# Expert tables of a decoder step: the second selection matrices move to ScalarE, and one ring of weight units runs through both tables

## The chip, the cores and the metric

The kernel runs on one core of a Trainium2 chip. The metric is the device time of one execution in microseconds; before the change the median of three runs was 3930.49 us (3925.4 to 3931.15).

## The reference

One inference step of one layer, all in fp32: a mixer (retention and gated linear attention) and then a product-key expert block, for 512 prompt tokens and 64 sample tokens. The change lies in the expert block:

```python
v1, i1 = lax.top_k(s1, 16); v2, i2 = lax.top_k(s2, 16)      # 8 heads, two halves of 128 keys
cand_s = v1[..., :, None] + v2[..., None, :]
cand_i = i1[..., :, None] * 128 + i2[..., None, :]
top_s, sel = lax.top_k(cand_s, 16)
eidx = take_along_axis(cand_i, sel)                          # 128 experts per token
gate = softmax(top_s)
act = gelu(einsum('thkd,td->thk', u_tab[eidx], xb))
out = einsum('thk,thkd->td', gate * act, v_tab[eidx])
```

There are 128 x 128 = 16384 experts, each with a row of 2048 numbers in the table u and one in the table v (128 MB a table).

## The kernel before

Of the 576 tokens, 384 are done densely: `experts_hidden` multiplies the whole table u with them, `outputs` the whole table v, and a matrix G of gates (one number for each expert and token, mostly zero) picks what counts. The other 192 tokens are done by gathers: GpSimd fetches the rows of 128 experts at a time with an indirect DMA of 1 MB, 192 gathers for each table.

**Units.** A table comes in 128 units of 1 MB (`Units`, lines 1483 to 1511). SyncE issues a unit's load (L1494), ScalarE rounds it to a high part (`split_hi`, L1501), VectorE forms the low part (`split_lo`, L1505), and TensorE multiplies with 48 matmuls of 384 columns (L1718 to L1720 for u, L2163 to L2165 for v). Two buffers each. Semaphores: `raw_in`, `hi_done`, `lo_done`, `unit_done`.

**First table (`experts_hidden`, names `hidden_...`).** Iteration n of the loop of each engine stands for unit n of 128. Units 0 to 39 go with the choice of the experts (`route`). From unit `first_gate` = 40 on, the gate matrices are built beside the units, 96 groups of 4 tokens: for each token a matrix `hot[1]` that has a one where iota equals the second key (GpSimd, L1662), a matrix `hot[0]` with the gate where iota equals the first key (VectorE, `firsts_hots`, L1930), a matmul of both (`gate_matrices`, L1703, awaits both), and a copy to a staging tile (`stage_gates`, ScalarE, L1759). After 8 groups SyncE stores 2 MB of G (`store_group`, L1606). Function `gate_groups(n)` says which groups unit n has: one, sometimes two. The buffers `hot` are double, so group k waits until group k-2 is multiplied (semaphore `made`). Every matmul group of a unit ends in a Gelu (L1773), whose result SyncE stores (192 KB, L1633), and only then issues the next load.

**Gathers and dots.** In iteration n GpSimd first builds its selection matrices and then issues the unit's gathers (L1649; 22 before unit 40, 170 after it, so one or two per unit), into 4 row buffers; VectorE multiplies each with the token's own row (`dot`, L1922) and so frees the buffer. VectorE's order in iteration n is: low part of unit n+1, `firsts_hots`, dots.

**Second table (`outputs`).** It is a block of its own; all engines meet at the boundary between blocks. SyncE then loads chunk 0 of the hidden values and of G (1.5 MB each, L2023 and L2025) and the first two units of v. VectorE clears the accumulators `acc` and `accg`, waits for the unit, multiplies the hidden chunk with G (L2088, 8 instructions), ScalarE rounds it (L2064, twice), VectorE forms the low part (L2095, twice), and TensorE may begin.

Of the kernel before, what the change touches and what calls it, by code (L numbers as in the profile page):

```python
# [1477 lines left out]
class Units:  # L1478
# [4 lines left out]
    def __init__(self, nc, a, per):  # L1483
        self.nc, self.per = nc, per
# [4 lines left out]
        self.hi_done, self.lo_done, self.done = a.sem("hi_done"), a.sem("lo_done"), a.sem("unit_done")  # L1489

# [6 lines left out]
    def split_hi(self, act, n, s):  # L1497
        act.wait_ge(self.raw_in[s], filled(n, s))

        wait(act, self.done, self.per * (n - 1))  # L1500
# [25 lines left out]
def experts_hidden(nc, name, c, ident, u_units, h_hi, h_lo, hidden, queries, keys, u_rows, h_rows, h_weight, expert_ids, dots, gates0, G):  # L1526
# [9 lines left out]
    first_gate, after_gates = 8 * TILES, NKEYS - 4  # L1536
# [16 lines left out]
    with ExitStack() as ctx:  # L1553
        a = Alloc(nc, ctx, name)
        un = Units(nc, a, 1)
# [6 lines left out]
        big = [a.sb(f"big{n}", [P, NKEYS * GT]) for n in range(2)]  # L1562
# [5 lines left out]
        picks_hot = spare[:].rearrange("p (k j) -> p k j", j=TOPK)  # L1568
        hot = [[spare[:, (2 * n + x) * P:(2 * n + x + 1) * P] for n in range(2 * B)] for x in range(2)]
# [23 lines left out]
            a.sem(x) for x in ("chosen", "back", "kept", "dstep", "ready", "ids_set"))  # L1593
        seconds_hot, firsts_hot, made, staged, row_used, carried, dot_gelu, weighted = (
# [6 lines left out]
        def _(sp):  # L1601
# [66 lines left out]
        def _(pe):  # L1668
# [27 lines left out]
            def gate_matrices(k):  # L1696
# [3 lines left out]
                pe.wait_ge(seconds_hot, B * (k + 1))  # L1700
# [31 lines left out]
        def _(act):  # L1732
# [12 lines left out]
            def keep(t):  # L1745
                act.wait_ge(back, t - 1)
                for n, x in enumerate(choices):
                    nc.scalar.copy(x[:, (t - 2) * P:(t - 1) * P], tg[:, n, :]).then_inc(kept, 1)
# [40 lines left out]
        def _(vec):  # L1789
# [144 lines left out]
            for n in range(NKEYS):  # L1934
                if n + 1 < NKEYS:
                    un.split_lo(vec, n + 1, (n + 1) % 2)
# [49 lines left out]
def outputs(nc, name, v_units, hidden, G, v_rows, expert_ids, dots, acc, accg):  # L1986
# [6 lines left out]
    with ExitStack() as ctx:  # L1993
        a = Alloc(nc, ctx, name)
        un = Units(nc, a, DT)
        gat = Gathers(nc, a, v_rows, expert_ids, NGATHER // (NCH // 2))
        W = a.sb("w", [P, CH, ND])
        Gc = a.sb("g", [P, NG, CH, GT])
# [4 lines left out]
        added, weighed, gated, w_in, w_hi_done, w_lo_done, w_set, cleared = (  # L2003
            a.sem(x) for x in ("added", "weighed", "gated", "w_in", "w_hi_done", "w_lo_done", "w_set", "cleared"))
# [12 lines left out]
        def _(sp):  # L2017
            def load_w(c):
# [3 lines left out]
                at = bass.ds(c, 1)  # L2022
                sp.dma_start(W[:].rearrange("p a t -> p (a t)"),  # L2023
                             hidden[at].rearrange("c p a t -> (c p) (a t)")).then_inc(w_in, 16)
                sp.dma_start(Gc[:].rearrange("p g a t -> p (g a t)"),  # L2025
# [330 lines left out]
```

## Time and profile before

| | |
|---|---|
| median of three runs | 3930.49 us |
| the profiled execution | 3937.12 us, its span 3935.3 us |
| TensorE busy | 3594.5 us (91%), mean granted clock 0.945 |
| VectorE, ScalarE, GpSimd busy | 2579.9, 1118.0, 1360.3 us |
| GpSimd's selection matrices (L1662) | 489.1 us |
| DMA | 965.63 MB, mean 245 GB/s |

Times are microseconds from the span's start. Matmuls overlap, so busy TensorE is not TensorE at its peak. A row of the timeline gives start, length, engine, line, operation, tiles, shapes and count, and in brackets the engine's idle time before it and what ended that.

### The profile page before, as it was taken

How to read it: one execution, taken by the hardware profiler on the slowest of the kernel's cores; microseconds unless marked ns; L12 is line 12 of the kernel's file. 1: busy time of each engine (PE TensorE's matmuls, PEld its weight loads, DVE VectorE, ACT ScalarE, POOL GpSimd, SP SyncE). 2: the span in 40 equal slices, each digit the busy share in tenths (PEclk: the TensorE clock that was granted, in tenths of full speed). 3: DMA queues.
4: the chain of work that ended last, by engine and by line, in shares of the span. 5: the costliest groups of instructions: out<-in, count | busy, mean ns of one | idle time of the engine just before them, and what ended most of it. 6: DMA issues, size and time to landing. Idle time of an engine off the chain costs nothing. (4 is left out here: it accounts for less than half of the span.)

```text
span 3935.3 us, 50012 instructions
## 1 busy us (share of the span) xinstructions
PE 3594.5 (91%) x19479; PEld 3341.1 (85%) x19479; DVE 2579.9 (66%) x3623; ACT 1118.0 (28%) x1130; POOL 1360.3 (35%) x993
## 2 busy tenths in 40 slices
PE   8999997886988989988998999998699999999996
PEld 6888886664877879888998999998699999999995
DVE  4111113885314138998777777777698989898996
ACT  5212112332214123322333333333122222222222
POOL 0000000000000000122978878888155545454451
PEclk9999998777999989998999999999799999999997
DMA  5222222534415143554888888988889898989986
GB/s 203 106 101 98 109 99 74 182 114 157 159 64 216 59 155 139 221 219 186 336 327 338 343 326 321 362 329 339 311 337 372 352 375 348 378 347 377 358 348 228
DMA packets 186998, 965.63 MB, mean 245 GB/s; under 512 B 18657, under 2 KB 61345, under 8 KB 86098
## 3 DMA queue, kind: packets, MB, share of 16 engines
q1 hardware_dynamic: 108082, 506.07, 34.1%
q0 software_dynamic: 61264, 426.27, 28.0%
q10 hardware_dynamic: 17488, 31.06, 2.2%
q8 instruction: 108, 1.77, 0.2%
q14 instruction: 56, 0.46, 0.0%
HBM read 865.77 MB, written 97.55 MB: 245 GB/s over the span
## 5 line engine op out<-in xcount | busy, mean ns | idle before, releaser
L1718 PE MATMUL hidden_hp<-dense_hi,hidden_whi 128*128 128x384 f32 x2048 | 712.8, 348 | 36.2 <-DVE hidden_wlo L1505 36.2
L2163 PE MATMUL outputs_vp<-outputs_w_hi,outputs_whi 128*128 128x384 f32 x2048 | 685.2, 335 | 36.1 <-DVE outputs_w_lo L2095 35.7
L1719 PE MATMUL hidden_hp<-dense_lo,hidden_whi 128*128 128x384 f32 x2048 | 700.0, 342 | 0.0
L1720 PE MATMUL hidden_hp<-dense_hi,hidden_wlo 128*128 128x384 f32 x2048 | 699.0, 341 | 0.0
L2164 PE MATMUL outputs_vp<-outputs_w_lo,outputs_whi 128*128 128x384 f32 x2048 | 684.7, 334 | 0.0
L2165 PE MATMUL outputs_vp<-outputs_w_hi,outputs_wlo 128*128 128x384 f32 x2048 | 684.6, 334 | 0.0
L1922 DVE CUSTOM_DVE_ANT_0 hidden_row<-hidden_row,hidden_h_row 128x2048 f32<-128x2048 f32 x192 | 439.1, 2300 | 157.8 <-DMA hidden_row<-u_rows,expert_ids 155.2
L1662 POOL TENSOR_SCALAR hidden_spare<-hidden_iota,hidden_seconds 128x128 f32<-128x128 f32 x384 | 489.1, 1286 | 133.4 <-PE hidden_tq L1703 88.1
L1649 POOL DMA_INDIRECT hidden_row<-u_rows,expert_ids x192 | 318.4, 1659 | 587.2 <-DVEq L1901 356.2
L1977 POOL DMA_INDIRECT outputs_row<-v_rows,outputs_id x192 | 315.9, 1645 | 554.3 <-DVE accg L2112 513.7
L2112 DVE SCALAR_TENSOR_TENSOR accg<-outputs_row,outputs_w_op,accg 128x2048 f32<-128x2048 f32 x192 | 450.8, 2348 | 52.1 <-DMA outputs_row<-v_rows,outputs_id 49.3
L1501 ACT CAST outputs_whi<-outputs_raw 128x2048 fp32r<-128x2048 f32 x128 | 245.1, 1915 | 794.3 <-PE outputs_vp L2165 643.2
L1718 PEld LDWEIGHTS hidden_hp<-dense_hi,hidden_whi 128*128 128x128 f32 x2048 | 398.3, 194 | 41.1 <-DVE hidden_wlo L1505 40.7
L2163 PEld LDWEIGHTS outputs_vp<-outputs_w_hi,outputs_whi 128*128 128x128 f32 x2048 | 384.9, 188 | 37.2 <-issue 37.0
L1719 PEld LDWEIGHTS hidden_hp<-dense_lo,hidden_whi 128*128 128x128 f32 x2048 | 397.6, 194 | 0.0
L1720 PEld LDWEIGHTS hidden_hp<-dense_hi,hidden_wlo 128*128 128x128 f32 x2048 | 396.1, 193 | 0.0
L2164 PEld LDWEIGHTS outputs_vp<-outputs_w_lo,outputs_whi 128*128 128x128 f32 x2048 | 385.0, 188 | 0.0
L2165 PEld LDWEIGHTS outputs_vp<-outputs_w_hi,outputs_wlo 128*128 128x128 f32 x2048 | 384.9, 188 | 0.0
L542 PE MATMUL in_proj_acc<-in_proj_whi,in_proj_rows_hi 128*128 128x512 f32 x960 | 376.1, 392 | 2.1 <-DVE in_proj_wlo L435 2.1
L1505 DVE TENSOR_TENSOR hidden_wlo<-hidden_raw,hidden_whi 128x2048 fp32r<-128x2048 f32 x128 | 294.3, 2300 | 121.9 <-ACT hidden_whi L1501 121.1
L1505 DVE TENSOR_TENSOR outputs_wlo<-outputs_raw,outputs_whi 128x2048 fp32r<-128x2048 f32 x128 | 293.4, 2292 | 56.2 <-ACT outputs_whi L1501 55.1
L548 PE MATMUL in_proj_acc<-in_proj_whi,in_proj_rows_lo 128*128 128x512 f32 x768 | 299.5, 390 | 0.0
(346 smaller groups left out, 5096.3 us busy)
## 6 DMA issues: line engine op xcount, KB each, us to landing
hidden_raw<-u_units SPq DMA_DIRECT2D x128, 1024.0 KB
outputs_raw<-v_units SPq DMA_DIRECT2D x128, 1024.0 KB
in_proj_raw<-w_in SPq DMA_DIRECT2D x48, 1024.0 KB
hidden<-hidden_hid SPq DMA_DIRECT2D x128, 192.0 KB
gate_mat<-hidden_big SPq DMA_DIRECT2D x12, 2048.0 KB
outputs_w<-hidden SPq DMA_DIRECT2D x16, 1536.0 KB
outputs_g<-gate_mat SPq DMA_DIRECT2D x16, 1536.0 KB
out_proj_raw<-w_out SPq DMA_DIRECT2D x16, 1024.0 KB, 7.5
```

Source lines behind the costliest of these rows:

```text
L542: nc.tensor.matmul(acc[t][:], hi_at(t, kk), whi[q][:, k, :], start=first, stop=False)
L1505: self.nc.vector.tensor_tensor(self.lo[s][:], self.raw[s][:], self.hi[s][:].bitcast(F32), ALU.subtract).then_inc(self.lo_done, 1)
L1649: pool.indirect_dma_start(row[g % U_ROWS][:], None, u_rows, bass.IndirectOffsetOnAxis(expert_ids[:, g:g + 1], 0)).then_inc(row_in[g % U_RO ...
L1662: nc.gpsimd.tensor_scalar(hot[1][B * (k % 2) + x], iota[:], seconds[:, at:at + 1], None, ALU.is_equal).then_inc(seconds_hot, 1)
L1718: mm(o, un.hi[s][:, x, :], h_hi[:, x, :], start=x == 0, stop=False)
L1719: mm(o, un.hi[s][:, x, :], h_lo[:, x, :], start=False, stop=False)
L1720: ins = mm(o, un.lo[s][:, x, :], h_hi[:, x, :], start=False, stop=x == KT - 1)
L1922: v.tensor_tensor_reduce(r[:], r[:], h_row[g % 3 // 2][:], 1.0, 0.0, mult, ALU.add, dots[:, g:g + 1]).then_inc(row_used, 1)
L2112: v.scalar_tensor_tensor(o[:], r[:], w_op[:, j:j + 1], o[:], mult, ALU.add).then_inc(gat.row_used, 1)
L2163: mm(o, un.hi[x][:, at, :], W_hi[s][:, e, :], start=e == 0, stop=False)
L2164: mm(o, un.hi[x][:, at, :], W_lo[s][:, e, :], start=False, stop=False)
L2165: ins = mm(o, un.lo[x][:, at, :], W_hi[s][:, e, :], start=False, stop=e == CH - 1)
```

## The change

Three things:

1. The matrices `hot[1]` are made by ScalarE: four activations |iota - second| and one Relu(1 - x) over all four (`seconds_hots`). The second keys are kept with their sign turned. ScalarE does it after the high part of unit n+1 and before it waits for unit n. GpSimd only issues gathers. The groups end three units earlier (`after_gates` 121 instead of 124).
2. `Units`, the two tiles `big` and the semaphore `w_in` are shared by both tables. The loads, high and low parts of the first units of v come in the loop of u; chunk 0 is loaded into `big` in iteration 126, after the last stores of G and the first of the hidden values have landed; SyncE no longer waits for G's stores at the block's end.
3. In `outputs` no accumulator is cleared (the first additions become copies), and the first unit is multiplied in two halves, each as soon as its half of the chunk is ready.

```diff
@@ experts_hidden: GpSimd
             for n in range(NKEYS):
-                if n == first_gate:
-                    pool.wait_ge(kept, 3 * (TILES - 2))
-                for k in gate_groups(n):
-
-                    wait(pool, made, k - 1)
-
-                    pool.sem_inc(carried, 1)
-                    for x in range(B):
-                        at = B * k + x
-                        nc.gpsimd.tensor_scalar(hot[1][B * (k % 2) + x], iota[:], seconds[:, at:at + 1], None,
-                                                ALU.is_equal).then_inc(seconds_hot, 1)
                 for g in gathers(n):
                     gather(g)
@@ experts_hidden: ScalarE
+            def seconds_hots(k):
+
+                wait(act, made, k - 1)
+                for x in range(B):
+                    at = B * k + x
+                    nc.scalar.activation(hot[1][B * (k % 2) + x], iota[:], ACT.Abs, bias=seconds[:, at:at + 1]).then_inc(seconds_off, 1)
+                act.wait_ge(seconds_off, B * (k + 1))
+                h = hots[:, k % 2, :, 1, :]
+                nc.scalar.activation(h, h, ACT.Relu, bias=1.0, scale=-1.0).then_inc(seconds_hot, 1)
...
-                if n + 1 < NKEYS:
-                    un.split_hi(act, n + 1, 1 - s)
+                un.split_hi(act, n + 1, 1 - s)
...
+                for k in gate_groups(n):
+                    seconds_hots(k)
                 act.wait_ge(un.done, n + 1)
@@ experts_hidden: SyncE
-                if n + 2 < NKEYS:
-                    un.load(sp, n + 2, s, u_units, n + 2)
+                un.load(sp, n + 2, s, *((u_units, n + 2) if n + 2 < NKEYS else (v_units, n + 2 - NKEYS)))
+                if n == NKEYS - 2:
+                    for x in range(2):
+                        sp.wait_ge(g_stored[x], 16 * NG // 2)
+                        sp.wait_ge(hid_stored[x], 16 * CH // 2)
+                    load_chunk(sp, big, w_in, hidden, G, 0)
...
             for s in range(2):
                 sp.wait_ge(hid_stored[s], 16 * NKEYS // 2)
-                sp.wait_ge(g_stored[s], 16 * NG // 2)
@@ experts_hidden
-    first_gate, after_gates = 8 * TILES, NKEYS - 4
+    first_gate, after_gates = 8 * TILES, NKEYS - 7
@@ outputs: VectorE
-            v.memset(acc[:], 0.0).then_inc(cleared, 1)
-            for x in accg:
-                v.memset(x[:], 0.0).then_inc(cleared, 1)
-            un.split_lo(vec, 0, 0)
-            for e in range(CH):
-                weigh(0, e)
-            weights_lo(0, 0, 0)
-            weights_lo(0, 0, 1)
-            vec.wait_ge(cleared, 3)
+            for x in range(2):
+                for e in range(HC):
+                    weigh(0, HC * x + e)
+                weights_lo(0, 0, x)
```

On ScalarE a unit with a group of gates stands so before, in its loop from unit 40 on (the cast is `split_hi`, `hidden_hid` the Gelu, the copy `stage_gates`):

```order
L1501 CAST hidden_whi<-hidden_raw 128x2048
L1773 ACTIVATE hidden_hid<-hidden_hp 128x384
L1759 COPY hidden_big<-hidden_tq 128x4x128
L1501 CAST hidden_whi<-hidden_raw 128x2048
L1773 ACTIVATE hidden_hid<-hidden_hp 128x384
```

The same place after the change (`hidden_spare` holds the matrices `hot`):

```order
L1509 CAST units_whi<-units_raw 128x2048
L1767 ACTIVATE hidden_spare<-hidden_iota,hidden_seconds 128x128 x4
L1770 ACTIVATE hidden_spare<-hidden_spare 128x4x128
L1799 ACTIVATE hidden_hid<-hidden_hp 128x384
L1781 COPY units_big<-hidden_tq 128x4x128
```

Five activations stand between the cast and the Gelu, and none of them is preceded by a table load there.

SyncE before, from the last store of G to the second chunk (the branches are the boundary between the blocks):

```order
L1606 DMA gate_mat<-hidden_big 128x16x256
L1633 DMA hidden<-hidden_hid 128x384 x3
L1553 UNCONDITIONAL_BRANCH
L2016 UNCONDITIONAL_BRANCH
L2023 DMA outputs_w<-hidden 128x3072
L2025 DMA outputs_g<-gate_mat 128x3072
L1494 DMA outputs_raw<-v_units 128x2048 x3
```

SyncE after the change, from the last loads of u to the same boundary:

```order
L1502 DMA units_raw<-u_units 128x2048
L1652 DMA hidden<-hidden_hid 128x384
L1502 DMA units_raw<-v_units 128x2048
L1537 DMA units_big<-hidden 128x3072
L1538 DMA units_big<-gate_mat 128x3072
L1652 DMA hidden<-hidden_hid 128x384
L1502 DMA units_raw<-v_units 128x2048
L1652 DMA hidden<-hidden_hid 128x384
L1568 UNCONDITIONAL_BRANCH
L2041 UNCONDITIONAL_BRANCH
```

Two units of v and chunk 0 have moved from behind the boundary to before it, between the last stores of hidden values.

## Rows read from the trace of the kernel before

**Rows 1.** Windows: length, busy PE, PEld, DVE, ACT, POOL, PEclk, DMA share, GB/s
```profile
1850.00:2786.00 936.00, 858.09 (x4995) 851.32 (x4995) 690.15 (x814) 303.56 (x276) 763.55 (x554) 0.95 0.87 332
2786.00:2817.60 31.60, 0.00 (x0) 0.00 (x0) 18.07 (x15) 6.64 (x4) 4.03 (x10) 0.52 0.74 299
2817.60:3880.70 1063.10, 1062.54 (x6116) 1061.75 (x6117) 950.16 (x730) 282.69 (x156) 526.68 (x374) 1.00 0.90 354
2172.00:2228.00 56.00, 56.00 (x345) 56.00 (x344) 38.26 (x47) 21.16 (x19) 47.03 (x38) 1.00 0.83 318
2228.00:2247.40 19.40, 12.81 (x62) 12.52 (x61) 17.30 (x19) 3.33 (x4) 13.48 (x10) 0.74 1.02 401
```

**Rows 2.** Timeline of ScalarE, the Gelu of six units from 1861 to 2782 us
```profile
1861.39 0.49 ACT L1773 ACTIVATE hidden_hid<-hidden_hp 128x384 f32<-128x384 f32 x1 [6.75 <-PE hidden_hp L1720]
...
2665.54 0.49 ACT L1773 ACTIVATE hidden_hid<-hidden_hp 128x384 f32<-128x384 f32 x1 [4.86 <-PE hidden_hp L1720]
...
2675.65 0.49 ACT L1773 ACTIVATE hidden_hid<-hidden_hp 128x384 f32<-128x384 f32 x1 [5.45 <-PE hidden_hp L1720]
...
2691.33 0.49 ACT L1773 ACTIVATE hidden_hid<-hidden_hp 128x384 f32<-128x384 f32 x1 [7.20 <-PE hidden_hp L1720]
...
2773.77 0.49 ACT L1773 ACTIVATE hidden_hid<-hidden_hp 128x384 f32<-128x384 f32 x1 [6.03 <-PE hidden_hp L1720]
2782.10 0.49 ACT L1773 ACTIVATE hidden_hid<-hidden_hp 128x384 f32<-128x384 f32 x1 [7.83 <-PE hidden_hp L1720]
```

**Rows 3.** Waits from 1850 to 2786 us: total, times, longest
```profile
DVE hidden_row L1922 <- DMA hidden_row<-u_rows,expert_ids: 155.2, 72, 8.0
...
PE hidden_tq L1703 <- DVE hidden_spare L1930: 68.0, 18, 7.4
```

**Rows 4.** GpSimd's groups from 1850 to 2786 us
```profile
L1662 POOL TENSOR_SCALAR hidden_spare<-hidden_iota,hidden_seconds 128x128 f32<-128x128 f32 x384 | 489.1, 1286 | 133.4 <-PE hidden_tq L1703 88.1 <-ACT hidden_gates L1748 42.7 <-issue 0.6
L1649 POOL DMA_INDIRECT hidden_row<-u_rows,expert_ids x170 | 274.4, 1614 | 62.0 <-issue 36.5 <-DVE dots L1922 24.8 <-PE hidden_tq L1703 0.6
```

**Rows 5.** Line L1662 (ns min/median/max), then timelines of GpSimd and VectorE from 2649 us
```profile
L1662 POOL TENSOR_SCALAR hidden_spare<-hidden_iota,hidden_seconds x384: 592/608/4881, 1851.8 to 2737.3; 128x128 f32<-128x128 f32 x192
...
2649.34 14.13 POOL L1662 TENSOR_SCALAR hidden_spare<-hidden_iota,hidden_seconds 128x128 f32<-128x128 f32 x7
2663.64 1.09 POOL L1649 DMA_INDIRECT hidden_row<-u_rows,expert_ids  x1 [0.16 <-issue]
...
2669.35 2.29 DVE L1922 CUSTOM_DVE_ANT_0 hidden_row<-hidden_row,hidden_h_row 128x2048 f32<-128x2048 f32 x1 [4.23 <-DMA hidden_row<-u_rows,expert_ids]
```

**Rows 6.** ScalarE's groups of the whole span that are nearest to the new instructions
```profile
L875 ACT ACTIVATE mixer_z_abs<-mixer_z_abs 128x512 f32<-128x512 f32 (+1 forms) x5 | 2.9, 588 | 0.1
...
L1780 ACT ACTIVATE hidden_gate<-hidden_gate 128x128 f32<-128x128 f32 x5 | 1.6, 311 | 0.1
```

**Rows 7.** Timelines of TensorE and VectorE in unit 87
```profile
2350.73 0.42 PE L1718 MATMUL hidden_hp<-dense_hi,hidden_whi 128*128 128x384 f32 x1
...
2353.90 2.29 DVE L1505 TENSOR_TENSOR hidden_wlo<-hidden_raw,hidden_whi 128x2048 fp32r<-128x2048 f32 x1 [1.43 <-ACT hidden_whi L1501]
...
2356.11 1.17 DVE L1930 TENSOR_SCALAR hidden_spare<-hidden_iota,hidden_firsts,hidden_gates 128x128 f32<-128x128 f32 x4
```

**Rows 8.** Timelines at the boundary of the tables: TensorE, SyncE, VectorE, ScalarE
```profile
2781.72 0.34 PE L1720 MATMUL hidden_hp<-dense_hi,hidden_wlo 128*128 128x384 f32 x1
...
2787.91 0.34 SPq L2023 DMA_DIRECT2D outputs_w<-hidden  x1
...
2810.45 3.83 DVE L2088 TENSOR_TENSOR outputs_w<-outputs_w,outputs_g 128x384 f32<-128x384 f32 x8
2814.20 3.42 DVE L2095 TENSOR_TENSOR outputs_w_lo<-outputs_w,outputs_w_hi 128x1536 fp32r<-128x1536 f32 x2
...
2812.44 1.47 ACT L2064 CAST outputs_w_hi<-outputs_w 128x1536 fp32r<-128x1536 f32 x1 [4.23 <-DVE outputs_w L2088]
...
2817.76 0.66 PE L2163 MATMUL outputs_vp<-outputs_w_hi,outputs_whi 128*128 128x384 f32 x1 [35.71 <-DVE outputs_w_lo L2095]
```

**Rows 9.** DMA queues, 2688 to 2691 us, behind a store of G: packets, MB, share
```profile
q0 software_dynamic: 148, 1.07, 84.7%
q1 hardware_dynamic: 155, 0.16, 14.9%
```

More of the change, by code:

```diff
@@ L1478, with __init__ @@
 class Units:
-    def __init__(self, nc, a, per):
-        self.nc, self.per = nc, per
+    def __init__(self, nc, a):
+        self.nc, self.first, self.per = nc, 0, 1
         self.raw = [a.sb(f"raw{s}", [P, KT, P]) for s in range(2)]
@@ L1489, in __init__, with turn_to, all_done @@
         self.hi_done, self.lo_done, self.done = a.sem("hi_done"), a.sem("lo_done"), a.sem("unit_done")
+    def turn_to(self, first, per):
+        self.first, self.per = first, per
+    def all_done(self, m):
+        return self.first + self.per * m
     def load(self, eng, n, s, table, at):
@@ L1498, in split_hi @@
         act.wait_ge(self.raw_in[s], filled(n, s))
-        wait(act, self.done, self.per * (n - 1))
+        wait(act, self.done, self.all_done(n - self.first - 1))
         self.nc.scalar.copy(self.hi[s][:], self.raw[s][:]).then_inc(self.hi_done, 1)
@@ L1983, in wait_row, with outputs @@
         return self.row[j % ROWS]
-def outputs(nc, name, v_units, hidden, G, v_rows, expert_ids, dots, acc, accg):
+def outputs(nc, name, un, big, w_in, v_units, hidden, G, v_rows, expert_ids, dots, acc, accg):
     mult = ALU.mult
@@ L2021, in load_w @@
                 wait(sp, w_lo_done, 2 * c)
[L2022 to L2025, printed above, removed]
[L2026 removed]
+                load_chunk(sp, big, w_in, hidden, G, c)
             def body(i):
@@ L2146, in _, with first_unit @@
             mm = nc.tensor.matmul
+            def first_unit():
+                for h in range(2):
+                    pe.wait_ge(w_lo_done, h + 1)
+                    for b in range(DT):
+                        o = vp[b][:, 0:ND]
+                        for e in range(HC * h, HC * (h + 1)):
+                            at = DT * e + b
+                            mm(o, un.hi[0][:, at, :], W_hi[0][:, e, :], start=e == 0, stop=False)
+                            mm(o, un.hi[0][:, at, :], W_lo[0][:, e, :], start=False, stop=False)
+                            ins = mm(o, un.lo[0][:, at, :], W_hi[0][:, e, :], start=False, stop=e == CH - 1)
+                        if h == 1:
+                            ins.then_inc(un.done, 1)
             def body(i):
@@ L2151, in body @@
                         n = unit(i, s, j)
-                        un.ready(pe, n)
-                        if j == 0:
+                        un.ready(pe, NKEYS + n)
+                        if j == 0 and not (isinstance(i, int) and i == s == 0):
                             pe.wait_ge(w_lo_done, 2 * (2 * i + s + 1))
                         x = j % 2
+                        if isinstance(i, int) and i == s == j == 0:
+                            first_unit()
+                            continue
                         for b in range(DT):
@@ L2287, in build @@
         with ExitStack() as rows:
-            dense = [sb(f"dense_{p}", [P, KT, ND], F32R, rows) for p in ("hi", "lo")]
+            dense = [rows.enter_context(nc.sbuf_tensor(f"dense_{p}", [P, KT, ND], F32R, side="right")) for p in ("hi", "lo")]
             project(nc, "queries", ident, None, sums, w["pq"], queries, w_col_dram=w["norm_ffn_cols"], squares=squares, row=h_rows,
                     dense=dense)
-            experts_hidden(nc, "hidden", consts, ident, tables["u_units"], *dense, hidden, queries, keys, tables["u_rows"], h_rows,
+            shared = Alloc(nc, ctx, "units")
+            un, big, w_in = Units(nc, shared), [shared.sb(f"big{n}", [P, NKEYS * GT]) for n in range(2)], shared.sem("w_in")
+            experts_hidden(nc, "hidden", consts, ident, un, big, w_in, tables["u_units"], tables["v_units"], *dense, hidden, queries, keys, tables["u_rows"], h_rows,
                            w["norm_ffn"], expert_ids, dots, gates0, G)
         acc, accg = sb("acc", [P, KT, ND]), [sb(f"accg{x}", [P, D]) for x in range(2)]
-        outputs(nc, "outputs", tables["v_units"], hidden, G, tables["v_rows"], expert_ids, dots, acc, accg)
+        outputs(nc, "outputs", un, big, w_in, tables["v_units"], hidden, G, tables["v_rows"], expert_ids, dots, acc, accg)
         finish(nc, "finish", ident, sums, w["norm_final"], acc, accg, outs["y"])
```

65 lines of the change are left out of this document (38 added, 27 removed).

## The prediction

> **What bounds the kernel now.** I read the windows first, since the share of a whole span hides its stages. The second table is at its end already: for 1063.1 us TensorE is busy 1062.54 us at clock 1.00 [rows 1]. What a change can win lies in front of it, in two places.
>
> The first is the stretch of the gate matrices, 1850 to 2786 us: 936 us, TensorE 858 us busy and at a clock of 0.95 [rows 1]. The pace is read from the Gelus, one for each unit. Two at the end, where no gates are built, stand 8.33 us apart (2773.77 and 2782.10). With two groups of gates in a unit it is 10.11 us (2665.54 to 2675.65), so a group costs TensorE (10.11 - 8.33) / 2 = 0.89 us. The next step is 15.68 us (to 2691.33) [rows 2]. Such a stall comes once in about seven units. From the Gelu of unit 40 (1861.39) to that of unit 127 (2782.10) are 920.7 us [rows 2]. TensorE alone would need 87 x 8.33 + 96 x 0.89 = 724.7 + 85.4 = 810.1 us. So 110.6 us are lost here.
>
> Who is late? TensorE waited 68.0 us in 18 waits for the matrices that VectorE makes, 7.4 us at the most; the rest of the loss is small waits, and TensorE's clock, which after idling is granted at the lower of its two levels (1.2 instead of 2.4 GHz) for a while: mean 0.74 in the stalled 19.4 us, 1.00 in the 56 us ahead of it. VectorE was late because it waited 155.2 us in 72 waits for gathered rows [rows 1, 3]. The rows were late because GpSimd issued them late: it is busy 763.55 of 936 us, and 489.1 us of that are the 384 selection matrices, 1286 ns each on the mean [rows 1, 4]. One takes 608 ns in the median and up to 4881 ns. From 2649.34 on seven of them took 14.13 us; the gather behind them was issued at 2663.64, and VectorE waited 4.23 us for a row until 2669.35 [rows 5]. While GpSimd was holding the gathers back, the transfers were not at their limit: share 0.83 in the 56 us ahead of a stall, 1.02 in the stall [rows 1]. The chain is GpSimd, gather, dot, matrices and low part, TensorE.
>
> The second place is the boundary: TensorE's last matmul of u ends at 2782.06, its first of v starts at 2817.76 after 35.71 us of idling [rows 8].
>
> **The change part by part.**
>
> *GpSimd.* It loses 489.1 us of 763.6. Left are 170 gathers with 274.4 us, 1.6 us each, and no wait for TensorE's `made` any more. Per unit that is some 3.1 us of 9.3. A gather now goes out as soon as a row buffer is free. So the 155.2 us of VectorE's waits have lost their cause as far as GpSimd is it.
>
> *ScalarE.* Per group it gains four activations of 128x128 and one of 128x512. The nearest rows are 311 and 588 ns [rows 6]: 4 x 0.311 + 0.588 = 1.83 us, with the wait for its own result I take 2.2 us; from below 1.8, from above 3.0 if each costs half as much again. In unit 87 TensorE starts at 2350.73, and VectorE starts the low part as ScalarE's cast ends, at 2353.90, that is 3.2 us into the unit [rows 7]. The new work runs from there to 5.4 us, with two groups to 7.6 us; TensorE asks for it at 8.33 us. It is hidden by the unit's own matmuls. Queued behind it stand only the Gelu, which waits for TensorE anyhow, and the copy. VectorE's own way from the cast is longer, 2.21 us low part and 1.1 us matrices [rows 7], so that way stays the last one. Cost 0; if the cover goes, because a load is late, both ways are late together and the longer one counts.
>
> *VectorE.* In this stretch 690 us busy [rows 1], nothing added but one low part. Per unit 7.8 us of some 9.3. It is not the bound.
>
> *Transfers.* They are moved, not reduced, and they are what is late next. The stretch moves 332 GB/s x 936 us = 310.8 MB at a share of 0.87, which is 814 us of all 16 engines [rows 1]. TensorE's own pace would ask for 99% of that. Into the same stretch come chunk 0 (3.1 MB) and one unit (1.05 MB): at 401 GB/s, the rate of a stretch at full share, 10.4 us. The sum is 825 us of transfers, against 1850 + 825 = 2675 at share 1.00. How near to 1.00 can it run? Below: 0.90, which the second table shows while TensorE never waits, so it is no limit. Above: 1.02 for 19.4 us with four gathers outstanding [rows 1]. I take 0.95, the middle, because each engine must wait at times for a buffer. Then TensorE's last matmul of u comes at 1850 + 825 / 0.95 = 2718. The ends are 2671 (TensorE's own floor, 2782 less 110.6) and 2767 (share 0.90).
>
> One row says how such a stretch can go wrong. Behind a store of G, whose packets are 1 KB, the gather's queue had 84.7% of the time and SyncE's 14.9% [rows 9]. The loads of units stand behind that store in SyncE's queue. There are 12 stores. Part of the missing 5% is this.
>
> *Boundary.* Block start came 2787.91 - 2782.06 = 5.85 us after the last matmul [rows 8]; this stays. Then chunk 0 is there, and half of the old work stands ahead of TensorE: 3.83 / 2 = 1.92 us (4 products), 1.47 us (cast), 3.42 / 2 = 1.71 us (low part) [rows 8], with two hand-overs some 5.3 us. The second half is ready another 5.2 us later, and the first half of the unit takes TensorE 24 matmuls, at half clock about as long: 0 to 1 us. The clears of the accumulators were in the shadow of the load and give nothing. The gap becomes 11.3 us instead of 35.7: 24.4 us less, if the chunk has landed. SyncE issues it at iteration 126, some 16 us before TensorE's end, in a stretch that is full; its transfer is in the 825 us above, so I don't count its lateness twice.
>
> *After the boundary.* The first three gathers of v were moved in the old gap. Now they meet the second chunk while TensorE works: 3.1 MB at 401 GB/s is 7.8 us, of which I count 2 (0 to 8). The copies in place of additions, the shared tiles and the sign of the second keys cost nothing on the path: same instructions in number and size.
>
> **Sum.** First matmul of v at 2718 + 11.3 + 2 = 2731 instead of 2817.8: 86 us less. 3937.1 - 86 = 3851 us for the profiled execution, which was 6.6 us above the median of the runs; so 3930.5 - 86 = 3844.5, and I say 3845 us. A measurement of this kernel tells 0.2%, 8 us, from nothing.
>
> The Trainium skill, "SBUF — State Buffer", section "A bandwidth-pool intuition that's wrong (but worth ruling out)", gives some 358 GB/s from HBM to one core and calls HBM almost always the bottleneck. By it 315 MB would take 880 us, the last matmul of u would come at 2730, and the gain would be 74 us. The trace shows 401 GB/s, though over 19.4 us only [rows 1].
>
> **The rivals.**
>
> *The transfers hold it at the rate of the second table.* For: 354 GB/s and share 0.90 were held there over 1063 us, and no long stretch shows more. Against: TensorE never waited there, so nothing asked for more; 1.02 was reached. Price: 315 MB at 354 GB/s = 890 us, last matmul at 2740, gain 64; or 825 / 0.90 = 917 us, last matmul at 2767, gain 37. Time 3867 to 3893. The sentence of the skill above would come out near this one. Chance 0.20.
>
> *TensorE gets its floor.* For: the stalls go with GpSimd's work, and the gathers run ahead with four buffers. Against: it needs the transfers at 0.99. Price: 110.6 + 24.4 = 135, time 3796 to 3810. Chance 0.13.
>
> *The stalls stay, only the boundary is better.* They were perhaps the transfers catching up: share 1.02 within them. Against: 0.83 ahead of each, with VectorE waiting for a gather not yet issued [rows 1, 5]. Price: 10 to 24 us, time 3906 to 3920. Chance 0.04.
>
> *Slower.* The loads of units starve. GpSimd no longer pauses, and each packet of 8 KB of a gather lets one of 1 KB of G pass: 148 to 155 in 3 us, 0.31 us each (0.847 x 3 x 16 / 131 packets of 8 KB) and 0.046 us each [rows 9]. Per DMA engine a store of G has 128 packets; if gathers never ceased they would take 128 x 0.31 us = 40 us, and the next load stands behind them. Four row buffers limit it: after 4 x 8 = 32 packets, 10 us, the queue of gathers is empty. From 9.2 us of delay per store on (110.6 / 12) the stretch wins nothing, and from 11.3 us on (with the 24.4 us of the boundary) the kernel is slower. By the four buffers that is 10 us until the gathers pause and 96 x 0.046 = 4.4 us for the rest, of which the load's slack of a unit takes most. Price at 14 us per store: 12 x 14 - 135 = 33 us, time 3963. Chance 0.03. Exactly the same within 8 us: 0.02.
>
> That the new activations need tables of their own is no rival: no load stands there in the order of ScalarE. The Trainium skill, "ScalarE: Activation LUTs", section "🔬 Table sets: the hidden batching unit", says as well that relu and abs are in every set; the loads that a trace of the changed kernel lists for that line would show it.
>
> **How the numbers follow.** Forecast (gain 65 to 110) 0.58, then 0.20, 0.13, 0.04, 0.03 and 0.02. The forecast's own range is 3820 to 3866. For 8 in 10 I reach up to 3886 and down to 3808. Faster by over 0.2%: 0.95; within: 0.02; slower: 0.03.
>
> **What the profile of the changed kernel would show.** GpSimd's L1662 gone and its busy time near 270 us in the stretch. VectorE's wait for gathered rows well under 155 us. TensorE's wait for the matrices of VectorE near zero; in its place small waits for the low part, which go back over the cast to loads of units, above all after a store of G. DMA share 0.93 to 0.97 up to the boundary, 360 GB/s or more. ScalarE's groups near 2 us, ending before TensorE's last matmul of the unit. A gap of 11 to 13 us at the boundary; if it is over 15, the chunk or the dots are late. What would make the prediction wrong: a share that stays at 0.90, or new stalls at the stores of G, or a wait in the first units of v.

## The result and the profile after

The changed kernel takes 3906.27 us in the median of six runs (3897.64 to 3912.61), the kernel before in the same comparison 3931.37 us. The ratio is 0.994, with a 95% interval from 0.9927 to 0.9953: 0.6% faster. The forecast was 3845 us, a gain of 86 us; it came to 25 us. The profiled execution took 3904.86 us (before 3937.12), its span is 3903.1 us. These two are 32 us apart, since the one before was 6 us above its median.

Where did the 32 us between the two profiled executions come from? The same two places as ahead of the change, windows of the changed kernel (length, busy PE, PEld, DVE, ACT, POOL, granted clock, DMA share, GB/s):

```profile
1850.00:2775.00 925.00, 847.75 (x4991) 843.92 (x4989) 676.90 (x815) 477.13 (x755) 272.99 (x167) 0.95 0.89 338
2770.00:2790.00 20.00, 4.81 (x19) 4.63 (x18) 10.35 (x15) 5.16 (x5) 6.75 (x10) 0.66 0.67 255
2789.50:3850.00 1060.50, 1060.06 (x6115) 1059.42 (x6114) 949.20 (x732) 283.62 (x157) 526.50 (x374) 1.00 0.90 356
```

They answer to [rows 1]. The second table is what it was. In the gate stretch GpSimd fell from 763.55 to 272.99 us, and yet the clock is still 0.95 and TensorE still waits. From the Gelu of unit 40 (1859.87) to that of unit 127 (2770.25) it is now 910.4 us, where it was 920.7 [rows 2]: 10 us gained of the 110.6 that were to be had. The boundary gave 20.5: TensorE waited 15.19 us there instead of 35.71 [rows 8].

The waits of the changed kernel from 1850 to 2790 us say what is late now (total, times, longest; [rows 3] before):

```profile
DVE units_wlo L1513 <- ACT units_whi L1509: 246.5, 85, 15.7
ACT units_whi L1509 <- DMA units_raw<-u_units: 95.8, 13, 14.0
...
PE hidden_tq L1710 <- DVE hidden_spare L1956: 62.0, 11, 9.8
```

VectorE no longer waits for a gathered row at all (155.2 us before). It waits for ScalarE's cast, and the cast waits 95.8 us, in 13 waits, for a load of a unit. That wait was 16.1 us before:

```profile
ACT hidden_whi L1501 <- DMA hidden_raw<-u_units: 16.1, 12, 3.6
```

TensorE's wait of 68.0 us for VectorE's matrices has become one of 62.0.

ScalarE's and SyncE's timelines from 2225 us on show one of the disturbances:

```profile
2225.27 0.49 ACT L1799 ACTIVATE hidden_hid<-hidden_hp 128x384 f32<-128x384 f32 x1 [3.64 <-PE hidden_hp L1727]
...
2235.39 1.90 ACT L1509 CAST units_whi<-units_raw 128x2048 fp32r<-128x2048 f32 x1 [8.08 <-DMA units_raw<-u_units]
...
2240.86 0.47 ACT L1799 ACTIVATE hidden_hid<-hidden_hp 128x384 f32<-128x384 f32 x1
...
2253.75 0.49 ACT L1799 ACTIVATE hidden_hid<-hidden_hp 128x384 f32<-128x384 f32 x1 [4.52 <-PE hidden_hp L1727]
...
2226.16 0.49 SPq L1502 DMA_DIRECT2D units_raw<-u_units  x1
...
2241.74 0.43 SPq L1502 DMA_DIRECT2D units_raw<-u_units  x1
```

The Gelus are 15.59 and then 12.89 us apart, where 9.21 and 10.11 are normal. The cast stood 8.08 us for its load. TensorE ran out of work at 2234.45 and went on at 2240.78, after 6.33 us. Behind the cast on ScalarE stood the Gelu of the unit that TensorE had finished; it started at 2240.86 with no wait of its own, and the next load, which SyncE issues after this Gelu, went out at 2241.74, some 6 us late. This second lateness costs nothing: the casts at 2245.46 and 2255.53 wait for no load. What makes the second step long is the clock, as the window of it shows:

```profile
2240.80:2253.80 13.00, 13.00 (x67) 13.00 (x68) 11.65 (x16) 6.28 (x11) 3.18 (x3) 0.79 0.73 255
```

TensorE is busy in all of it, at a mean granted clock of 0.79: from 2239.4 to 2246.3, after the idling, it was granted the lower of its two levels (1.2 instead of 2.4 GHz). So one late load makes two long steps, the first by waiting, the second by the clock.

All 22 steps of over 10.6 us in the stretch of the gates are such pairs, behind 11 of the 12 stores of G. In the second of a pair the cast waits 0.7 us at the most for its load, TensorE idles 2.5 us at the most, and the clock is at the lower level for 3.4 to 8.1 us. The one store without a pair is the second, at 2002.5 us: it landed after 15.0 us, and only 212 packets of gathers passed beside it, where 630 passed beside the store at 2208.2.

Around the last store of G, 2708 to 2738 us (packets, MB, share of the engines' time; then the issues of this window with the median time to landing):

```profile
q0 software_dynamic: 874, 6.34, 50.9%
q1 hardware_dynamic: 2856, 5.41, 50.0%
...
gate_mat<-units_big SPq DMA_DIRECT2D x1, 2048.0 KB, 26.8
```

The store of 2 MB took 26.8 us to land, though 16 engines were busy all the time. How the two queues share them is seen in the store at 2208.2 us; the first two rows are 2216 to 2218 us, the others 2220 to 2222 us:

```profile
q0 software_dynamic: 105, 0.73, 87.0%
q1 hardware_dynamic: 103, 0.10, 14.7%
...
q1 hardware_dynamic: 706, 0.72, 101.5%
q0 software_dynamic: 11, 0.03, 4.1%
```

While gathers are under way one packet of G passes for one of theirs; when they pause, G has the engines for itself. By the trace's packets, those of the store pass in 15 to 18 us in 11 of the 12 stores, beside 436 to 550 packets of 8 KB of gathers (four row buffers have 512), and in 8.5 us beside 75 in the second. The page of the changed kernel has 22.5 us as the median of the twelve stores, and 6.3 us for a load of a unit:

```profile
units_raw<-u_units SPq DMA_DIRECT2D x128, 1024.0 KB, 6.3
...
gate_mat<-units_big SPq DMA_DIRECT2D x12, 2048.0 KB, 22.5
```

The boundary, in the changed kernel's timelines of SyncE, VectorE and TensorE; the first row is the last store of hidden values:

```profile
2770.76 0.34 SPq L1652 DMA_DIRECT2D hidden<-hidden_hid  x1
...
2779.95 1.98 DVE L2105 TENSOR_TENSOR units_big<-units_big 128x384 f32<-128x384 f32 x4 [6.15 <-PEq L120]
2783.47 1.78 DVE L2112 TENSOR_TENSOR outputs_w_lo<-units_big,outputs_w_hi 128x1536 fp32r<-128x1536 f32 x1 [1.54 <-ACT outputs_w_hi L2082]
...
2785.40 0.66 PE L2174 MATMUL outputs_vp<-outputs_w_hi,units_whi 128*128 128x384 f32 x1 [15.19 <-DVE outputs_w_lo L2112]
```

The block starts near 2779.9, 9 us after that store was issued, and from there to TensorE it is 5.5 us.

ScalarE's new work is as foretold. From its groups, 1850 to 2775 us:

```profile
L1767 ACT ACTIVATE hidden_spare<-hidden_iota,hidden_seconds 128x128 f32<-128x128 f32 x384 | 122.8, 398 | 0.0
...
L1770 ACT ACTIVATE hidden_spare<-hidden_spare 128x512 f32<-128x512 f32 x96 | 60.8, 633 | 3.0
```

That is 1.9 us for a group, by the busy time, and no table load stands at these lines in the trace. In the normal units it ends 3.6 us before the Gelu, whose bracket in the first timeline row above shows that gap.

### The profile page after: what moved, and what is told of

It is laid out like the page before. It is cut to its first block and busy times, and to the rows that moved or that the text cites. A ratio compares the mean times of both kernels' runs of the same rounds, so it can differ in the third digit from the quotient of the medians.

```text
span 3903.1 us, 50109 instructions
## 1 busy us (share of the span) xinstructions
PE 3586.4 (92%) x19479; PEld 3335.9 (85%) x19479; DVE 2555.1 (65%) x3620; ACT 1290.1 (33%) x1610; POOL 878.6 (23%) x609
## 5 line engine op out<-in xcount | busy, mean ns | idle before, releaser
L1513 DVE TENSOR_TENSOR units_wlo<-units_raw,units_whi 128x2048 fp32r<-128x2048 f32 x256 | 586.2, 2290 | 335.8 <-ACT units_whi L1509 334.3
L1509 ACT CAST units_whi<-units_raw 128x2048 fp32r<-128x2048 f32 x256 | 491.8, 1922 | 864.4 <-PE outputs_vp L2200 624.1
L1725 PE MATMUL hidden_hp<-dense_hi,units_whi 128*128 128x384 f32 x2048 | 709.9, 347 | 41.5 <-DVE units_wlo L1513 41.5
L1726 PE MATMUL hidden_hp<-dense_lo,units_whi 128*128 128x384 f32 x2048 | 697.6, 341 | 0.0
L1727 PE MATMUL hidden_hp<-dense_hi,units_wlo 128*128 128x384 f32 x2048 | 695.9, 340 | 0.0
L2198 PE MATMUL outputs_vp<-outputs_w_hi,units_whi 128*128 128x384 f32 x2032 | 678.9, 334 | 0.4 <-DVE units_wlo L1513 0.4
L2200 PE MATMUL outputs_vp<-outputs_w_hi,units_wlo 128*128 128x384 f32 x2032 | 678.7, 334 | 0.0
L2199 PE MATMUL outputs_vp<-outputs_w_lo,units_whi 128*128 128x384 f32 x2032 | 678.7, 334 | 0.0
L1725 PEld LDWEIGHTS hidden_hp<-dense_hi,units_whi 128*128 128x128 f32 x2048 | 395.9, 193 | 46.4 <-DVE units_wlo L1513 46.0
L1726 PEld LDWEIGHTS hidden_hp<-dense_lo,units_whi 128*128 128x128 f32 x2048 | 395.4, 193 | 0.0
## 6 DMA issues: line engine op xcount, KB each, us to landing
gate_mat<-units_big SPq DMA_DIRECT2D x12, 2048.0 KB, 22.5
units_big<-gate_mat SPq DMA_DIRECT2D x16, 1536.0 KB, 15.7
```

What stands on the lines that cost most here:

```text
L1509: self.nc.scalar.copy(self.hi[s][:], self.raw[s][:]).then_inc(self.hi_done, 1)
L1513: self.nc.vector.tensor_tensor(self.lo[s][:], self.raw[s][:], self.hi[s][:].bitcast(F32), ALU.subtract).then_inc(self.lo_done, 1)
L1725: mm(o, un.hi[s][:, x, :], h_hi[:, x, :], start=x == 0, stop=False)
L1726: mm(o, un.hi[s][:, x, :], h_lo[:, x, :], start=False, stop=False)
L1727: ins = mm(o, un.lo[s][:, x, :], h_hi[:, x, :], start=False, stop=x == KT - 1)
L2198: mm(o, un.hi[x][:, at, :], W_hi[s][:, e, :], start=e == 0, stop=False)
```

## The experiments

Theory A, after this reading: gathers now go out as soon as a row is free, and by turns each of their packets of 8 KB lets one packet of SyncE's queue through. A store of G has 2048 packets of 1 KB, so it holds that queue for some 15 to 18 us, and the loads of units stand behind it. Its second half, tested with `loads_early`: a late cast holds back the Gelu, and with it the issue of the next load. Theory B, the forecast's own: the transfers as a whole are near their limit. Theory C: ScalarE's added work is itself late.

In the text below "the stretch" is the time from the Gelu of unit 40 to that of unit 127 in the profiled execution (before 920.7, changed 910.4, TensorE alone 810.1 us).

### Each half of the change alone

`ring_only` is the changed kernel with the selection matrices back on GpSimd (and with them TensorE's wait and the sign of the second keys):

```diff
             for n in range(NKEYS):
...
+                for k in gate_groups(n):
+
+                    wait(pool, made, k - 1)
+
+                    pool.sem_inc(carried, 1)
+                    for x in range(B):
+                        at = B * k + x
+                        nc.gpsimd.tensor_scalar(hot[1][B * (k % 2) + x], iota[:], seconds[:, at:at + 1], None,
+                                                ALU.is_equal).then_inc(seconds_hot, 1)
                 for g in gathers(n):
...
-                for k in gate_groups(n):
-                    seconds_hots(k)
```

> The changed kernel with the second selection matrices back on GpSimd, as before the change. Theory A (the first table gained little, because a store of G now blocks the loads of units; the boundary gained by itself): the gate stretch runs as before, some 920 us from the Gelu of unit 40 to that of unit 127, and the boundary keeps its 20 us: 3910 us. Rival (the matrices gave nothing but cost ScalarE time): no slower than the changed kernel's 3906 us, perhaps faster.

Measured: 3944.54 us against 3928.04, ratio 1.0043 (1.0029 to 1.0057). It is slower than the kernel before, which neither theory had. Its boundary is as good as that of the changed kernel (TensorE waits 15.7 us), but its stretch is 944.8 us.

`act_only` is the kernel before with ScalarE's `seconds_hots` in place of GpSimd's loop, and nothing else; the groups end where they did. Of its edit the call in ScalarE's loop:

```diff
...
                     un.split_hi(act, n + 1, 1 - s)
+                for k in gate_groups(n):
+                    seconds_hots(k)
```

> The kernel before with the second selection matrices on ScalarE alone: no common ring, the old boundary, groups until three units before the end as before. Theory A: some 10 us less in the gate stretch and nothing at the boundary, 3920 us; in the trace VectorE waits for no gathered row, and ScalarE waits some 95 us for loads of units, nearly all behind stores of G. Rival (ScalarE's new work is late by itself): such waits are spread over all units and the time is 3930 us or more.

Measured: 3910.84 us, ratio 0.9955 (0.9938 to 0.9972), as Theory A had it to within 10 us. The stretch is 898.8 us. VectorE waits for no gathered row, the casts wait 82.6 us in 10 waits for loads from 1850 to 2700 us, and the pairs of long steps lie around the stores of G. The rest of the change, then, is worth 5 us by the medians and 8 by the profiled executions: 20.7 at the boundary, less 11.6 that the stretch grew, less 1 from before unit 40.

`squeeze` asks what made the stretch grow. It is the kernel before with one number changed:

```diff
-    first_gate, after_gates = 8 * TILES, NKEYS - 4
+    first_gate, after_gates = 8 * TILES, NKEYS - 7
```

> The kernel before with one number changed: the 96 groups of gates end three units earlier (after_gates 121 instead of 124), as the change has it. The run with the ring and GpSimd's matrices was 16 us slower than before though its boundary was 20 us better; its gate stretch was 945 us instead of 921. Theory (GpSimd is the limit there, and more groups for each unit are more than it can do): the stretch is some 940 us here too, the kernel 3945 to 3955 us. Rival (the early loads and the chunk of the ring take the time): no change, 3930 us.

Measured: 3957.99 us, ratio 1.0066 (1.005 to 1.0082), the stretch 952.4 us: 32 us more than before, a little over what was expected (26 us by the medians; its profiled execution is 8 us above its median). So the earlier end of the groups is enough to make `ring_only` slow, and the early loads are not needed for it. With GpSimd as the limit, 96 groups in 81 units in place of 84 cost some 26 to 32 us.

With the matrices on ScalarE the stretch of the changed kernel is 11.6 us longer than that of `act_only`. Their Gelus tell where: from unit 40 to unit 123 both take 863.8 us, and all of the 11.6 us lies behind, in the two steps of 16.31 and 13.66 us behind the last store of G. In `act_only` that store goes out at 2734.7 us and no long step follows it. So on ScalarE the denser groups cost nothing, but their earlier end puts the last store ahead of loads that are still awaited.

### The store of G

`g_queue` changes who issues the twelve stores. Bytes, packets, and the order against the staging copies are the same; SyncE's loop loses them, ScalarE's gets them. Each store also goes out some microseconds earlier (the first at 1919.7 instead of 1927.1 us):

```diff
                 for k in gate_groups(n):
                     stage_gates(k)
+                    if (k + 1) * B % GT == 0:
+                        g = (k + 1) * B // GT - 1
+                        act.wait_ge(staged, k + 1)
+                        act.dma_start(G[:, :, g].rearrange("c p a t -> p c (a t)"),
+                                      stage[g % 2].rearrange("p (c a) t -> p c (a t)", a=CH)).then_inc(g_stored[g % 2], 16)
```

> The changed kernel with the 12 stores of G issued by ScalarE, so in a queue of their own, not ahead of the loads of units. Theory A (queue order: 1 KB packets of G pass one for one with 8 KB packets of gathers, the loads stand behind them): the waits for loads fall from 96 us to under 30, the Gelus of units 40 to 127 from 910 to some 840 us, the kernel to 3840 us. Rival B (the transfers as a whole are at their limit, share 0.89 to 0.95 is all there is): same bytes and packets, so no change, 3900 to 3910 us, the waits only move. Rival C (ScalarE's selection matrices behind its cast are what is late): no change either, but with the DMA share below 0.9 in the stalls.

Measured: 3807.03 us, ratio 0.9691 (0.9675 to 0.9707): 99 us less than the changed kernel by the medians, 33 us less than I had expected of it. The stretch is 811.5 us, TensorE's own time to within 2 us. A window in it, once for this kernel and once for the changed one:

```profile
1862.00:2670.00 808.00, 806.95 (x4924) 805.97 (x4923) 663.81 (x800) 475.64 (x744) 294.67 (x165) 1.00 0.98 381
```

```profile
1862.00:2670.00 808.00, 752.83 (x4465) 749.61 (x4463) 599.10 (x739) 435.65 (x700) 241.21 (x149) 0.96 0.90 343
```

In the same 808 us the transfers moved 381 instead of 343 GB/s, and their share rose from 0.90 to 0.98. Theory B falls: nothing was at a limit at 0.90. Theory C falls too, since ScalarE makes the same matrices in the same place. The queues of `g_queue` in this window:

```profile
q0 software_dynamic: 23883, 173.93, 53.1%
q1 hardware_dynamic: 24820, 107.74, 35.7%
q10 hardware_dynamic: 24768, 25.17, 8.8%
...
ACT units_whi L1509 <- DMA units_raw<-u_units: 24.2, 19, 4.3
```

The stores have a queue of their own, q10. On the page of this run each takes 46.4 us in the median to land (40.6 in `g_queue_again`), and nobody stands behind it. It then lies beside the loads of some five units and no step is over 10.6 us, so the earlier moment of issue is not what helps. The casts wait 24.2 us for loads, 4.3 at the most (last row, waits from 1850 to 2690 us).

The Trainium skill, "DMA: Bandwidth & Descriptors", section "Issuing engines are not separate DMA queues", says that issuing from several engines saves only the time on the sequencer. The runs here do not agree: the same transfers issued by another engine are in another queue, and the time is 99 us less.

`g_long` leaves the stores with SyncE and makes their packets large. Each partition's 16 KB go to one run of G. The gates are then not where the second table reads them, so the output differs; bytes, waits and loads are the same.

```diff
-                sp.dma_start(G[:, :, g].rearrange("c p a t -> p c (a t)"),
-                             stage[x].rearrange("p (c a) t -> p c (a t)", a=CH)).then_inc(g_stored[x], 16)
+                sp.dma_start(G.rearrange("c p g a t -> (c p g a t)").rearrange("(g p x) -> g p x", g=NG, p=P)[g],
+                             stage[x].rearrange("p a t -> p (a t)")).then_inc(g_stored[x], 16)
```

> The changed kernel with each store of G written as runs of 16 KB for each partition instead of 1 KB (its places in G are then not those that the second table reads, so the output's gates are shuffled; bytes, waits and loads are the same). Theory A: a store has 256 packets of 8 KB or so, each pass lets as many bytes through as a gather, the loads behind it come 10 us earlier; waits for loads under 30 us and 3840 us. Rival B (bytes are the limit): the packets of G took 71 us of all engines and would take some 60, so at the most 10 us less. Rival C: no change.

Measured: 3841.75 us, ratio 0.9779 (0.9763 to 0.9795), the stretch 845.9 us. A store lands in 15.2 instead of 22.5 us. The time is as expected, the waits for loads are 54.8 us and not under 30: 2 MB in front of a load cost something even in large packets. The size of the packets is about two thirds of what the stores cost, 65 of 99 us.

### Before the change

`before_gq` makes the same edit to the kernel before.

> The kernel before, GpSimd's selection matrices and the old boundary, with only the stores of G moved to ScalarE's queue. Theory A (before the change GpSimd was the limit, and its pauses let the stores through): little, 3915 to 3928 us, with the stalls of once in seven units still there and VectorE still waiting some 150 us for rows. Rival (the stores ahead of the loads were the cause of the stalls before the change too): the stalls go without touching GpSimd, 3850 us or less.

Measured: 3931.81 us, ratio 1.0009 (0.9999 to 1.0019): no difference, and 4 us above the range expected. The stretch is 918.4 us, VectorE still waits 175.8 us for rows, and the long steps are there, ten of them at the same units as before (55, 62, 69, 76, 83, 90, 104, 111, 118, 125). So they were not the stores' doing. While GpSimd is the limit the place of the stores costs nothing. Its pauses let them through: in 6 of the 12 stores of the kernel before, the packets of G passed in 6 to 7 us, with at most 62 packets of 8 KB of gathers beside them.

`act_gq` is `act_only` with the same edit, so both without ring and new boundary.

> The kernel before with two edits: selection matrices on ScalarE and the stores of G in ScalarE's queue; old boundary. Theory A: the gate stretch reaches TensorE's floor of 810 us as in the run with the whole change; the boundary is the old 36 us instead of 17.5, so some 18 to 20 us more than that run: 3825 us. Rival (the common ring of units gives more than the boundary): over 3835 us.

Measured: 3825.99 us, ratio 0.9737 (0.972 to 0.9755). Stretch 809.6 us, the boundary wait 35.9 us. Against `g_queue` it is 19 us slower, as the boundary alone would make it. The four medians make a table:

| | G behind SyncE's loads | G in a queue of its own |
|---|---|---|
| matrices on GpSimd | 3930.65 | 3931.81 |
| matrices on ScalarE | 3910.84 | 3825.99 |

Neither edit does much alone; together they are worth 105 us. (`act_only` was measured against 3928.04 us, so its own gain is 17 us.)

### The order of the loads, and who else stands in a queue

`loads_early` issues each load one place earlier in SyncE's loop, ahead of the wait for the Gelu; the stores of G stay.

```diff
+            un.load(sp, 2, 0, u_units, 2)
             for n in range(NKEYS):
                 s = n % 2
-                un.load(sp, n + 2, s, *((u_units, n + 2) if n + 2 < NKEYS else (v_units, n + 2 - NKEYS)))
+                if n + 1 < NKEYS:
+                    un.load(sp, n + 3, 1 - s, *((u_units, n + 3) if n + 3 < NKEYS else (v_units, n + 3 - NKEYS)))
```

> The changed kernel with every load of a unit issued one place earlier in SyncE's order: as soon as its buffer is free, ahead of the wait for the unit's Gelu, not behind it. Each disturbance of the changed kernel is two long steps, some 16 and 13 us. Theory A with its second half (the cast that waits for a late load holds back the Gelu behind it on ScalarE, and the next load waits for that Gelu): the second long step of each pair goes and the first gets shorter, since the load has 3 us more; the Gelus of units 40 to 127 come to 850 to 880 us, the kernel to 3860. Rival (only the place behind the store of G matters): the load still stands behind the store, pairs stay, 3900 us.

Measured: 3851.36 us, ratio 0.9797 (0.9778 to 0.9816), the stretch 841.9 us; the kernel is 9 us and the stretch 8 us below what Theory A had, and not for its reason. Long steps in pairs are still there, behind six of the stores, now two units apart (13.54 us to unit 77, 12.84 us to unit 79); in the second TensorE was again granted the lower clock, for 3.41 us. The first half of Theory A stands, its second half falls: the next load's issue was not what made the second step. The waits from 1850 to 2700 us show that the victim changed:

```profile
ACT hidden_hid L1801 <- DMA hidden<-hidden_hid: 55.6, 8, 12.8
ACT units_whi L1509 <- DMA units_raw<-u_units: 9.4, 7, 2.2
```

The casts wait 9.4 us for loads (15.8 up to 2790 us, where the changed kernel has 95.8). Now Gelus wait 55.6 us for a store of hidden values to land and free its buffer, and that store stands behind the store of G in the same queue. Outside the stretch this kernel lost 25 us: before unit 40 the loads of queries came to stand behind a later wait, TensorE waited 35.5 us for them, and unit 40's Gelu is at 1885.07 instead of 1859.87.

`gq_stores` is `g_queue` with the 128 stores of hidden values issued by ScalarE too, right behind each Gelu.

> The changed kernel with the stores of G and the 128 stores of hidden values both issued by ScalarE. For the boundary: it now comes 12 us after TensorE's last matmul, not 5.85, and SyncE waits there for the last store of hidden values, which stands behind a load of v. Theory (queue order again): in a queue of its own that store lands in 3 us, the boundary comes 2 to 4 us earlier, 3804 us. Rival (the last two dots, 3 us after TensorE, set it): no more than 1 us. Against both: ScalarE has 128 issues of 0.35 us and as many waits more, which its slack should hide.

Measured: 3829.18 us, ratio 0.9748 (0.973 to 0.9765), 22 us slower than `g_queue`, where I had expected 3 us faster. At the boundary it was right: TensorE waits 14.2 us instead of 17.5. But the stretch is 832.3 us. ScalarE's line of the Gelu:

```profile
L1794 ACT ACTIVATE hidden_hid<-hidden_hp x128: 472/490/494, 1442.9 to 2691.6; 128x384 f32<-128x384 f32 x128
...
  DMA hidden<-hidden_hid: 19.4, 2
```

Two Gelus waited 19.4 us for stores, which now stood behind a store of G in ScalarE's queue. It is the same fault as in the changed kernel, made again in the other queue. A second cost is in the issues themselves:

```profile
1991.38 6.11 ACTq L1796 DMA_DIRECT2D hidden<-hidden_hid  x1
```

Eight stores of hidden values took ScalarE 2.8 to 6.1 us to issue, each the next one behind a store of G, 28.6 us in all, where the others take some 0.35; the copy behind the one shown started at 1997.59. I had counted 0.35 for each. SyncE's issues behind a store of G are long in the changed kernel too (3.83 and 2.51 us at 2216.57 and 2220.45), and none of either engine is over 1.2 us in `g_queue`. Why an issue takes longer there no run shows.

`tail` is `g_queue` with only the last two stores of hidden values on ScalarE, when no store of G is left.

> The run with the stores of G in ScalarE's queue, and in addition the last two stores of hidden values (units 126 and 127) issued there. Theory (at the boundary SyncE waits 8.3 us for the last store, which stands in its queue behind chunk 0 and a load of v): the gap falls from 17.5 to some 14 us, without the stalls that all 128 stores in that queue brought: 3 us less than its sister run on the same chip. Rival (the last dots and chunk 0 set it): the same within 1 us.

> The kernel of the run g_queue once more, to be compared on one chip with the run tail. All theories: 3807 us within 4.

Measured on one chip, five rounds: `tail` 3806.66 us (3805.45 to 3807.95), `g_queue_again` 3809.16 us (3806.65 to 3810.44), ratios to before 0.9682 (0.9669 to 0.9696) and 0.9688 (0.9675 to 0.9702). TensorE's wait at the boundary is 16.0 instead of 17.8 us. The direction is as expected; the difference of 2.5 us is within what these runs scatter, so `tail` and `g_queue` count as equal. Both beat the changed kernel by 2.5%.

## Why the prediction was wrong

**What bounds the kernel before: right.** GpSimd was the limit. Taking its matrices away took VectorE's waits for rows from 155.2 us to none, and `squeeze` shows the other side: more groups for each unit cost 32 us.

**GpSimd, ScalarE, VectorE: right.** 272.99 us of GpSimd left where I had 274.4; 1.9 us for a group on ScalarE within 1.8 to 3.0, ahead of TensorE's need; VectorE was not the bound.

**Transfers: the step that failed.** I wrote that the sum of the transfers "are what is late next", took a share of 0.95 (the middle of my 0.90 and 1.02 is 0.96), and put TensorE's last matmul of u at 2718. It came at 2770. The volume was no limit: `g_queue` moves the same bytes at a share of 0.98 over 808 us. What was late was one kind of transfer, the loads, for their place in a queue. I had the row for it [rows 9] and put its price at a part of "the missing 5%". Of the three signs of being wrong that I named two came: the share stayed at 0.89 to 0.90, and there are new stalls at the stores of G. The number alone would have misled: my rival with the share of 0.90 had the last matmul at 2767, 3 us from what came, and its cause is refuted by `g_queue`.

The rival with a chance of 0.03, "slower", had the right mechanism and the right order of size. Its bound by four row buffers held: I had 14 us for a store, and the packets of G take 15 to 18. It said that from 9.2 us per store on the stretch wins nothing. Measured, the stretch lost 100.3 us to TensorE's floor, 8.4 us for each of 12 stores. Where it went wrong is its clause that the load's slack takes most of the 14 us. In the 63 units whose loads went out beside no store the cast starts 4.1 us after its load has landed, in the median; that is all the slack there was, and the casts waited 95.8 us, 8 for each store. TensorE idled 72.5 us in the stretch, which is 6.0 for each. The other 27 us are the clock, which I had named for the kernel before and left out of the price of a store. They show in TensorE's busy time for the same 4944 matmuls from the Gelu of unit 40 to that of unit 127, first the changed kernel, then `g_queue`:

```profile
1859.87:2770.25 910.38, 837.88 (x4944) 834.05 (x4942) 667.49 (x802) 471.26 (x746) 271.12 (x165) 0.95 0.90 340
...
1861.43:2672.95 811.52, 810.43 (x4944) 809.13 (x4942) 666.30 (x802) 476.56 (x746) 294.67 (x165) 1.00 0.98 381
```

The Trainium skill's 358 GB/s, weighed there as a rival limit, was passed by 381 GB/s over 808 us (all queues, reads and writes together).

**Boundary: right in kind, 4 us too good.** I had a gap of 11.3 us (its terms, 5.85 and 5.3, add to 11.2); it was 15.2. The work after the block's start took 5.5 us where 5.3 were foretold: its first product starts at 2779.95 and TensorE at 2785.40. The start itself came 9.7 us after the last matmul instead of 5.85. SyncE waited 6.0 us there for the last store of hidden values, behind a load of v; before it waited 1.6. With that store in the other queue `gq_stores` and `tail` have gaps of 14.2 and 16.0 us, where `g_queue` has 17.5 and 17.8.

**After the boundary: right.** In the second table TensorE waits 0.4 us in all for a unit; it is busy 1060.06 of 1060.5 us. The 2 us taken for it were not needed.

**The sum.** Of 86 us foretold, the boundary was to give 24.4 less 2 and gave 20.5; the stretch was to give 64 and gave 10. The rest of the 32 us between the profiled executions, 1.5 us, is from before unit 40.

What stays open: why an issue behind a store of G takes up to 6 us, and what part of the lateness of a load comes from that and what from the queue.

## What to carry to other kernels

When an engine that issued transfers is relieved, look at each queue for what its pauses had let through: a large store in small packets ahead of a load that someone waits for did no harm here while the other queues paused. Add the transfers by queue and by who stands behind whom, not only by bytes; here the bytes fitted and the order cost 99 us. Add what the clock takes after a wait: here 27 us on top of 72 us of waiting. And two edits that do little alone (0 and 17 us) can be worth 105 together, so an edit that showed no gain against the old bound should be tried again once the bound has moved.

## What the runs showed that I had not expected

The 16 DMA engines ran at a share of 0.98, 381 GB/s, for 808 us, with TensorE waiting less than 2 us in that time. Moving the twelve stores of 2 MB to the queue of another issuing engine raised their own landing time from 22.5 to 46.4 us and took 99 us off the kernel. An issue that stands behind such a store in its queue held its engine for up to 6.11 us instead of some 0.35.
